# Retention scores and retained values as three fp32r passes of high and low parts, with two tiles moved in memory

## The chip, the cores and the metric

One core of a Trainium2 chip runs the whole program in one launch. The metric is the device time in microseconds (us). TensorE multiplies; its products land in eight PSUM banks. VectorE (DVE), ScalarE (ACT) and GpSimd (POOL) work on tiles in SBUF, and the queue of SyncE (SP) issues most transfers. Each engine takes its own instructions strictly in the order in which they are written.

## The reference

The model is an encoder trunk over two requests, a prompt of 256 and a sample of 512 tokens, 1024 wide, with two layers. Layer 0 mixes by retention, layer 1 by neighbourhood attention; each is followed by a mixture of 16 experts and a gated embedding. What the change touches is the retention mixer, here without the chunks in which the reference writes it:

```python
q, k, v, g = split(h @ w_in)                 # 4 heads; q, k 256 wide, v, g 512 wide
q = rope(q); k = rope(k) * 256 ** -0.5
scores = (q @ k.T) * decay                   # decay falls with the distance, both directions
o = scores @ v
o = (o - mean(o)) * rsqrt(var(o) + 1e-6) * gn_w
out = (silu(g) * o) @ w_out
```

## The kernel before

The retention stage is the first, at about 40 to 700 us. Its work is cut into eight units, one for each head and request, in the order of `UNITS` (line 33): units 0, 2, 4 and 7 are prompt units (2 tiles of 128 tokens), units 1, 3, 5 and 6 sample units (4 tiles). Weights come in chunks through `raw`; ScalarE casts a chunk to fp32r, its high part (`high_of_chunk`, line 604), and VectorE subtracts that from the original, which gives the low part (`low_of_chunk`, line 613). A dense product is then made of three fp32r matmuls, high by high, low by high, high by low (`part_products`, line 1443). A chunk's parts lie in one of two places, so that its cast waits until TensorE has used the chunk before the last.

For each unit TensorE runs, in this order: values (`two_chunks("v", ...)`, line 1480), scores (line 1485), the first half of the gates (`g0`, line 1490), the retained values `o` (line 1499), the second half of the gates (`g1`) with the transposes of the gated rows between its tiles (line 1506), the next unit's queries and keys (line 1519), and the unit's output (`o0`, `o1`, line 1527). Scores and `o` go through `product` (line 1375) in plain fp32; all other products of the stage through `part_products`. In units 0 and LAST (7) transposes of normed rows stand before and after the scores (`norm_columns`), and in LAST the router's logits and the choice of the experts' tokens for the sample (`eight_best`) lie between the steps.

The other engines have hand-written orders of their own. ScalarE (lines 1062 to 1116) casts chunks, copies values from PSUM to `r_v` (line 1091), takes the SiLU of the gates (line 1104) and casts the transposed rows (line 1067). VectorE (lines 1976 to 2047) subtracts low parts, turns queries and keys (`rotary`, line 1839) straight into `r_qk`, scales scores by the decay strip into `r_s` (`decayed`, line 1855), takes mean and variance of `o` (`centred`), multiplies by the gates into `r_og` (`gated`), subtracts for the low part of the transposed rows (`transposed`, into `r_ot`), and adds outputs to `resid` (`added`). `scaled` and `norm_low` make normed rows and their low parts, behind squares on ScalarE (line 1015) and roots on GpSimd (lines 858 and 859). PSUM banks are dealt in turn over the list of `ret_keys` (line 151): a product waits until the product eight places before it has been read out.

Of the kernel before, what the change touches and what calls it, by code (L numbers as in the profile page):

```python
# [21 lines left out]
P = 128  # L22
D = 1024
# [248 lines left out]
def build(nc, x_prompt, x_sample, p_prompt, p_sample, ret_w_in, ret_decay_logit, ret_gn_w, ret_w_out,  # L272
# [4 lines left out]
    with ctx:  # L277
# [29 lines left out]
        xn_first = [put(f"xn_first{t}", [P, D], 64 + 4 * t) for t in range(TT)]  # L307
        xn_mid = [put(f"xn_mid{t}", [P, D], kb) for t, kb in enumerate((176, 180, 60, 68, 168, 192))]
# [6 lines left out]
        r_qk = put("r_qk", [P, 4, SEQ_S], 48)  # L315
        r_v = put("r_v", [P, 4, RET_DV], 56)
        r_s = put("r_s", [P, 4, SEQ_S], 64)
        r_ot = [put(f"r_ot{k}", [P, 4, SEQ_S], 72 + 8 * k, F32R) for k in range(2)]
# [180 lines left out]
        ret_rot = sem("ret_rot")  # L499
# [495 lines left out]
        def _(act):  # L995
# [58 lines left out]

            for t in range(2):
                squares(0, t)
# [5 lines left out]
            for u in range(len(UNITS)):  # L1062
# [19 lines left out]
                if u == 0:  # L1082
                    squares(0, 4)
                    squares(0, 5)
# [4 lines left out]
                for t in range(nt):  # L1089
                    b, done = filled(act, "ret", ("v", u, t))  # L1090
                    nc.scalar.copy(r_v[:, t, :], b[:, :]).then_inc(done, 1)
                if u in (0, LAST):
                    for t in GROUP_TILES[1]:
                        norm_high(int(u == LAST), t)
                split_ret("g1", u)
# [17 lines left out]
                if u < LAST:  # L1113
                    if new_head(u + 1):
# [251 lines left out]
        def _(pe):  # L1366
# [8 lines left out]
            def product(phase, key, lhs, rhs, i=0, m=P):  # L1375

                b, full = fill(pe, phase, key, i)
                n = rhs[0].shape[-1]
                for c, (x, y) in enumerate(zip(lhs, rhs)):
                    last = nc.tensor.matmul(b[0:m, 0:n], x, y, start=(c == 0), stop=(c == len(lhs) - 1))  # L1380
                last.then_inc(full, 1)

# [94 lines left out]
            for u in range(len(UNITS)):  # L1477
# [5 lines left out]
                pe.wait_ge(ret_rot, 2 * u + 2)  # L1483
                for t in range(nt):
                    product("ret", ("s", u, t), [r_qk[:, 2 + k, t * P:(t + 1) * P] for k in range(2)],
                            [r_qk[:, k, 0:n] for k in range(2)])
# [8 lines left out]
                for t in range(nt):  # L1495
                    drained(pe, "ret", ("v", u, t))
                    drained(pe, "ret", ("s", u, t))
                for t in range(nt):
                    product("ret", ("o", u, t), [r_s[:, k, t * P:(t + 1) * P] for k in range(nt)],
                            [r_v[:, k, :] for k in range(nt)])  # L1500
# [870 lines left out]
```

## Time and profile before

| | before |
|---|---|
| three runs | 2460.53, 2458.11, 2456.77 us; median 2458.11 |
| profiled execution | 2456.45 us, its span 2454.8 us |
| TensorE busy | 2367.5 us, 96% of the span |
| VectorE busy | 1742.6 us, 71% |
| ScalarE busy | 1337.0 us, 54% |
| GpSimd busy | 298.8 us, 12% |
| mean granted TensorE clock | 0.985 |

The profile is that of one execution. Busy shares are means over stages with different limits; what ended last in a stage is read from the chain of waits, which is followed back from the last instruction. Matmuls overlap one another, so the mean duration of one is longer than the pace at which they follow each other; the pace is read from the chain, whose pieces join without overlap.

### The profile page before, as it was taken

The numbers are of one execution on the slowest core, as the hardware profiler recorded it, in microseconds if no ns is written. First come the engines' busy times: TensorE is split into PE (matmuls) and PEld (weight loads), VectorE is DVE, ScalarE is ACT, GpSimd is POOL, SyncE is SP. The second block draws the span as 40 slices with busy tenths as digits, with TensorE's granted clock in tenths as the row PEclk, the third lists the DMA queues.
The fourth block names the chain that finished last, engine by engine and source line by source line (L and its number), as shares of the span: only waits on it lengthen the run. The fifth ranks groups of instructions, "written<-read, shape, count | busy, mean of one in ns | idle before, by whom it ended". The sixth has DMA issues, their size and how long they took to land.

```text
span 2454.8 us, 33887 instructions
## 1 busy us (share of the span) xinstructions
PE 2367.5 (96%) x11934; PEld 1934.6 (79%) x11934; DVE 1742.6 (71%) x1989; ACT 1337.0 (54%) x1454; POOL 298.8 (12%) x360
## 2 busy tenths in 40 slices
PE   8999999999979999999999999998889999999997
PEld 6878788687768888888878888886678888888876
DVE  6545455344679888888866677766578888888854
ACT  4223222222447777777764455444157777777762
POOL 1000000000111221112111101000111111121011
PEclk9999999999989999999999999998889999999999
DMA  6424324132499999999972533332599999999931
GB/s 235 132 72 126 108 96 149 59 107 72 157 345 395 389 392 392 394 389 390 388 193 56 134 102 99 93 93 73 170 339 393 392 394 390 389 392 392 356 125 43
DMA packets 210961, 577.27 MB, mean 235 GB/s; under 512 B 24384, under 2 KB 65856, under 8 KB 210752
## 3 DMA queue, kind: packets, MB, share of 16 engines
q1 hardware_dynamic: 193584, 526.35, 57.5%
q0 software_dynamic: 17296, 49.83, 8.0%
q8 instruction: 53, 0.87, 0.1%
q14 instruction: 28, 0.23, 0.0%
HBM read 547.80 MB, written 30.43 MB: 236 GB/s over the span
## 4 chain that ended last, share of the span: by engine, by line
PE 91%; DVE 3%; DMA 3%; issue 1%; ACT 1%; POOL 0%; SPq 0%; DVEq 0%; POOLq 0%; ACTq 0%
PE bank L1557 43%; PE bank L1443 38%; PE bank L1372 4%; PE bank L1380 4%; PE bank L1743 1%; PE bank L1725 1%; DMA rows_normed<-xn_late 1%; DVE d_parts L613 1%; DMA m_x<-rows_normed,idx_t 1%; DMA resid<-in_x_sample 0%; DMA rows_summed<-m_y,idx_out 0%; DMA raw<-in_ret_w_in 0%; DVE top_i L1946 0%; DVE m_at L1948 0%; DMA resid<-rows_summed 0%
## 5 line engine op out<-in xcount | busy, mean ns | idle before, releaser
L2080 DVE TENSOR_TENSOR w_parts<-wt,w_parts 128x2048 fp32r<-128x2048 f32 x384 | 874.5, 2289 | 133.7 <-ACT w_parts L1133 125.3
L1133 ACT CAST w_parts<-wt 128x2048 fp32r<-128x2048 f32 x384 | 734.2, 1913 | 195.0 <-PE bank L1557 184.4
L1557 PE MATMUL bank<-w_parts,m_xt 128*128 128x512 f32 x2976 | 689.0, 390 | 2.1 <-ACT m_y L1191 2.1
L1557 PEld LDWEIGHTS bank<-w_parts,m_xt 128*128 128x128 f32 x2976 | 556.1, 188 | 117.2 <-issue 2.9
L1443 PE MATMUL bank<-d_parts,xt 128*128 128x512 f32 (+1 forms) x1872 | 388.0, 364 | 4.4 <-DVE d_parts L613 4.4
L1557 PE MATMUL bank<-w_parts,m_hidt 128*128 128x512 f32 x1632 | 382.7, 394 | 2.8 <-DVE m_hidt L2072 2.8
L1443 PEld LDWEIGHTS bank<-d_parts,xt 128*128 128x128 f32 x1872 | 316.0, 190 | 62.3 <-issue 7.4
L1557 PEld LDWEIGHTS bank<-w_parts,m_hidt 128*128 128x128 f32 x1632 | 306.1, 189 | 66.0 <-issue 3.3
L604 ACT CAST d_parts<-raw 128x512 fp32r<-128x512 f32 (+1 forms) x168 | 183.3, 1107 | 245.5 <-PE bank L1443 237.4
L613 DVE TENSOR_TENSOR d_parts<-raw,d_parts 128x512 fp32r<-128x512 f32 (+1 forms) x168 | 215.5, 1296 | 134.8 <-ACT d_parts L604 134.3
L1443 PE MATMUL bank<-xt,d_parts 128*128 128x256 f32 (+1 forms) x1536 | 284.1, 340 | 7.0 <-DVE xt L1803 2.9
L1443 PEld LDWEIGHTS bank<-xt,d_parts 128*128 128x128 f32 x1536 | 235.4, 189 | 37.5 <-issue 8.0
L1443 PE MATMUL bank<-e_w,xt 128*128 128x512 f32 x576 | 133.6, 391 | 0.0
L1443 PE MATMUL bank<-d_parts,r_ot 128*128 128x512 f32 x576 | 132.3, 390 | 0.0
L1443 PEld LDWEIGHTS bank<-d_parts,r_ot 128*128 128x128 f32 x576 | 107.6, 188 | 22.9 <-DVE r_ot L1891 0.2
L1443 PEld LDWEIGHTS bank<-e_w,xt 128*128 128x128 f32 x576 | 107.3, 188 | 21.9
L905 POOL DMA_INDIRECT m_x<-rows_normed,idx_in x26 | 86.6, 3330 | 21.9 <-POOL idx_in L902 19.5
L2242 DVE CUSTOM_DVE_ANT_0 n_s<-bank,n_b 128x256 f32<-128x256 f32 (+1 forms) x96 | 44.6, 465 | 57.6 <-PE bank L1725 55.4
L902 POOL COPY idx_in<-idx_t 96x1 uint32 x26 | 19.6, 755 | 531.1 <-PE bank L1372 531.1
L858 POOL TENSOR_SCALAR meansq<-mv 128x1 f32<-128x1 f32 x24 | 4.6, 192 | 551.5 <-DVE mv L1871 551.5
L1104 ACT ACTIVATE r_tmp<-bank 128x512 f32<-128x512 f32 x24 | 14.4, 599 | 102.9 <-PE bank L1443 102.9
L1380 PE MATMUL bank<-r_v,r_s 128*128 128x512 f32 x160 | 70.2, 593 | 0.0
(184 smaller groups left out, 2035.6 us busy)
## 6 DMA issues: line engine op xcount, KB each, us to landing
wt<-in_exp_w_gate SPq DMA_DIRECT2D x128, 1024.0 KB, 14.2
wt<-in_exp_w_up SPq DMA_DIRECT2D x128, 1024.0 KB, 13.1
wt<-in_exp_w_down SPq DMA_DIRECT2D x128, 1024.0 KB, 13.3
raw<-in_ret_w_in SPq DMA_DIRECT2D x32, 1024.0 KB, 5.2
raw<-in_na_w_in SPq DMA_DIRECT2D x24, 1024.0 KB, 5.4
raw<-in_ret_w_in SPq DMA_DIRECT2D x32, 512.0 KB, 4.5
raw<-in_ret_w_out SPq DMA_DIRECT2D x16, 1024.0 KB, 5.1
raw<-in_ple_w_gate SPq DMA_DIRECT2D x8, 1024.0 KB, 8.1
```

Source lines behind the costliest of these rows:

```text
L604: nc.scalar.copy((d_parts[:, b, 0, :] if dst is None else dst)[:, cols], raw[:, b, cols]).then_inc(part_h, 1)
L613: nc.vector.tensor_tensor(low[:, cols], raw[:, b, cols], high[:, cols].bitcast(F32), ALU.subtract)\
L905: nc.gpsimd.indirect_dma_start(out=m_x[:, :], out_offset=None, in_=rows_normed[l], in_offset=bass.IndirectOffsetOnAxis(ap=rows, axis=0)).t ...
L1133: nc.scalar.copy(w_parts[c % RING][:, 0, :], wt[:, place // 2, place % 2 * 2048:place % 2 * 2048 + 2048])\
L1372: last = nc.tensor.transpose(b[:, c * w:(c + 1) * w], src, ident[0:k, 0:k])
L1380: last = nc.tensor.matmul(b[0:m, 0:n], x, y, start=(c == 0), stop=(c == len(lhs) - 1))
L1443: ins = nc.tensor.matmul(b[0:m, 0:rhs.shape[-1]], lhs, rhs, start=(first and j == 0 and wk == xk == 0), stop=(last and j == tiles - 1 and ...
L1557: last = nc.tensor.matmul(b[:, :], lhs[x][:, 2 * k + j, :], w[:, part, j, f * HALF:(f + 1) * HALF], start=(k == j == 0 and x == part == 0) ...
L1725: last = nc.tensor.matmul(b[:, 0:nk * P], n_qk[qk][rows, h // 2, t * P:(t + 1) * P], n_qk[kk][rows, 2 + h // 2, k0 * P:(k0 + nk) * P], sta ...
L1743: last[k] = nc.tensor.matmul(o_bank[k * NA_DH:(k + 1) * NA_DH, h // 2 * P:(h // 2 + 1) * P], n_v[:, k0 + j, (h + k) * NA_DH:(h + k + 1) * ...
L2080: v.tensor_tensor(w_parts[c % RING][:, 1, :], wt[:, k // 2, k % 2 * 2048:k % 2 * 2048 + 2048], w_parts[c % RING][:, 0, :].bitcast(F32), AL ...
L2242: v.tensor_tensor_reduce(out=n_s[:, u % 2, 0:w], in0=b[:, 0:w], in1=n_b[:, u % 2, 0:w], scale=-1.0, scalar=-3 * MASKED, op0=ALU.add, op1=A ...
```

## The change

Scores and retained values are made by `part_products` too, in three fp32r matmuls in place of one fp32 product, and `product` goes away. `rotary` writes `r_qk_full`; ScalarE casts it into `r_qk` (`queries_high`), VectorE subtracts (`queries_low`, in place, into `r_qk_low`). `decayed` writes `r_s_full`; ScalarE casts it tile by tile into `r_s[0]` (`scores_high`), VectorE subtracts in place into `r_s[1]` (`scores_low`). The values' copy becomes a cast into `r_v[0]`, and VectorE subtracts from the bank into `r_v[1]` (`values_low`), which now is what frees the bank. TensorE waits for `ret_qk_low` in place of `ret_rot`, and for `ret_s_low` in place of the emptied score banks. In memory `r_ot` moves to the places of `r_s`, `r_qk_full` and `r_qk_low` share those of `r_og`, and two tiles each of `xn_first` and `xn_mid` move.

```diff
-        xn_first = [put(f"xn_first{t}", [P, D], 64 + 4 * t) for t in range(TT)]
-        xn_mid = [put(f"xn_mid{t}", [P, D], kb) for t, kb in enumerate((176, 180, 60, 68, 168, 192))]
+        xn_first = [put(f"xn_first{t}", [P, D], kb) for t, kb in enumerate((64, 68, 72, 76, 60, 84))]
+        xn_mid = [put(f"xn_mid{t}", [P, D], kb) for t, kb in enumerate((176, 180, 60, 84, 168, 192))]
...
-        r_qk = put("r_qk", [P, 4, SEQ_S], 48)
-        r_v = put("r_v", [P, 4, RET_DV], 56)
-        r_s = put("r_s", [P, 4, SEQ_S], 64)
-        r_ot = [put(f"r_ot{k}", [P, 4, SEQ_S], 72 + 8 * k, F32R) for k in range(2)]
+        r_qk = put("r_qk", [P, 4, SEQ_S], 48, F32R)
+        r_qk_low = [[put(f"r_qk_low{g}{j}", [P, 2, GROUPS[g][1]], 184 + (2, 8)[g] * j, F32R) for j in range(2)]
+                    for g in range(2)]
+        r_v = [put(f"r_v{k}", [P, 4, RET_DV], (56, 80)[k], F32R) for k in range(2)]
+        r_s = [put(f"r_s{k}", [P, 4, SEQ_S], 64 + 8 * k, F32R) for k in range(2)]
+        r_qk_full = [[put(f"r_qk_full{g}{j}", [P, 2, GROUPS[g][1]], 184 + (2, 8)[g] * j) for j in range(2)]
+                     for g in range(2)]
+        r_s_full = put("r_s_full", [P, 4, SEQ_S], 72)
+        r_ot = [put(f"r_ot{k}", [P, 4, SEQ_S], 64 + 8 * k, F32R) for k in range(2)]
...
# ScalarE
+            def queries_high(u):
+                g, n = unit(u)[1], unit(u)[3]
+                for j in range(2):
+                    act.wait_ge(ret_rot, 2 * u + j + 1)
+                    nc.scalar.copy(r_qk[:, 2 * j:2 * j + 2, 0:n], r_qk_full[g][j][:, :, :])\
+                        .then_inc(ret_qk_high, 1)
+            def scores_high(u):
+                n, nt = unit(u)[3:]
+                for t in range(nt):
+                    drained(act, "ret", ("s", u, t))
+                    nc.scalar.copy(r_s[0][:, t, 0:n], r_s_full[:, t, 0:n]).then_inc(ret_s_high, 1)
...
                 split_ret("v1", u)
                 if u == 0:
+                    queries_high(0)
                     squares(0, 4)
                     squares(0, 5)
...
                 for t in range(nt):
-                    b, done = filled(act, "ret", ("v", u, t))
-                    nc.scalar.copy(r_v[:, t, :], b[:, :]).then_inc(done, 1)
+                    b, _ = filled(act, "ret", ("v", u, t))
+                    nc.scalar.copy(r_v[0][:, t, :], b[:, :]).then_inc(ret_v_high, 1)
                 if u in (0, LAST):
                     for t in GROUP_TILES[1]:
                         norm_high(int(u == LAST), t)
+                scores_high(u)
                 split_ret("g1", u)
...
                 split_ret("o1", u)
                 if u < LAST:
+                    queries_high(u + 1)
                     if new_head(u + 1):
                         strip_exp(u + 1)
                     split_ret("v0", u + 1)
...
# TensorE
-                pe.wait_ge(ret_rot, 2 * u + 2)
+                pe.wait_ge(ret_qk_low, 2 * u + 2)
+                queries = [r_qk[:, 0:2, 0:n], r_qk_low[g][0]]
+                keys = [r_qk[:, 2:4, 0:n], r_qk_low[g][1]]
                 for t in range(nt):
-                    product("ret", ("s", u, t), [r_qk[:, 2 + k, t * P:(t + 1) * P] for k in range(2)],
-                            [r_qk[:, k, 0:n] for k in range(2)])
+                    part_products([x[:, :, t * P:(t + 1) * P] for x in keys], lambda k, a, j: queries[k][:, j, :], "ret",
+                                  [("s", u, t)], 2, lambda a: slice(0, P), True, True)
...
                 for t in range(nt):
                     drained(pe, "ret", ("v", u, t))
-                    drained(pe, "ret", ("s", u, t))
+                pe.wait_ge(ret_s_low, tiles_before(u) + nt)
                 for t in range(nt):
-                    product("ret", ("o", u, t), [r_s[:, k, t * P:(t + 1) * P] for k in range(nt)],
-                            [r_v[:, k, :] for k in range(nt)])
+                    part_products(r_v, lambda k, a, j: r_s[k][:, j, t * P:(t + 1) * P], "ret", [("o", u, t)], nt, None,
+                                  True, True)
...
# VectorE: rotary writes r_qk_full[g][j], decayed writes r_s_full; new:
+            def queries_low(u):
+                g, n = unit(u)[1], unit(u)[3]
+                for j in range(2):
+                    dve.wait_ge(ret_qk_high, 2 * u + j + 1)
+                    v.tensor_tensor(r_qk_low[g][j][:, :, :], r_qk_full[g][j][:, :, :], r_qk[:, 2 * j:2 * j + 2, 0:n].bitcast(F32), ALU.subtract)\
+                        .then_inc(ret_qk_low, 1)
+            def values_low(u):
+                for t in range(unit(u)[4]):
+                    b, done = filled(dve, "ret", ("v", u, t))
+                    dve.wait_ge(ret_v_high, tiles_before(u) + t + 1)
+                    v.tensor_tensor(r_v[1][:, t, :], b[:, :], r_v[0][:, t, :].bitcast(F32), ALU.subtract).then_inc(done, 1)
+            def scores_low(u):
+                n, nt = unit(u)[3:]
+                for t in range(nt):
+                    dve.wait_ge(ret_s_high, tiles_before(u) + t + 1)
+                    v.tensor_tensor(r_s[1][:, t, 0:n], r_s_full[:, t, 0:n], r_s[0][:, t, 0:n].bitcast(F32), ALU.subtract)\
+                        .then_inc(ret_s_low, 1)
...
                 low_ret("v1", u)
                 if u == 0:
+                    queries_low(0)
...
                 low_ret("g0", u)
+                values_low(u)
...
                 decayed(u)
+                scores_low(u)
                 low_ret("g1", u)
...
                 for t in range(nt):
                     added(u, t, 0)
+                queries_low(u + 1)
                 low_ret("v0", u + 1)
...
             low_ret("g0", LAST)
+            values_low(LAST)
             for t in (4, 5):
                 scaled(1, t)
...
             for t in (4, 5):
                 norm_low(1, t)
+            scores_low(LAST)
             low_ret("g1", LAST)
```

## Rows read from the trace of the kernel before

**Rows 1.** The page: busy times, and the chain that ended last.
```profile
PE 2367.5 (96%) x11934; PEld 1934.6 (79%) x11934; DVE 1742.6 (71%) x1989; ACT 1337.0 (54%) x1454; POOL 298.8 (12%) x360
...
PE 91%; DVE 3%; DMA 3%; issue 1%; ACT 1%; POOL 0%; SPq 0%; DVEq 0%; POOLq 0%; ACTq 0%
PE bank L1557 43%; PE bank L1443 38%; PE bank L1372 4%; PE bank L1380 4%; PE bank L1743 1%; PE bank L1725 1%; DMA rows_normed<-xn_late 1%; DVE d_parts L613 1%; DMA m_x<-rows_normed,idx_t 1%; DMA resid<-in_x_sample 0%; DMA rows_summed<-m_y,idx_out 0%; DMA raw<-in_ret_w_in 0%; DVE top_i L1946 0%; DVE m_at L1948 0%; DMA resid<-rows_summed 0%
```

**Rows 2.** Chain in order of time, units 2 to 4: start us, us, what.
```profile
239.37 43.58 PE bank L1443 x192
282.95 6.87 PE bank L1380 x16
289.82 10.89 PE bank L1443 x48
300.71 13.73 PE bank L1380 x32
...
326.34 0.61 ACT r_tmp L1104
...
327.08 5.99 PE bank L1443 x48
...
371.93 1.73 PE bank L1380 x8
```

**Rows 3.** Groups by shape: line, operation, count, busy us, mean ns, idle before.
```profile
L1443 PEld LDWEIGHTS bank<-d_parts,xt 128*128 128x128 f32 x1872 | 316.0, 190 | 62.3 <-issue 7.4 <-DVE d_parts L613 4.8
...
L1443 PE MATMUL bank<-d_parts,r_ot 128*128 128x512 f32 x576 | 132.3, 390 | 0.0
...
L1380 PE MATMUL bank<-r_v,r_s 128*128 128x512 f32 x160 | 70.2, 593 | 0.0
L613 DVE TENSOR_TENSOR d_parts<-raw,d_parts 128x512 fp32r<-128x512 f32 x104 | 68.9, 683 | 0.5 <-ACT d_parts L604 0.5
L604 ACT CAST d_parts<-raw 128x512 fp32r<-128x512 f32 x104 | 61.0, 611 | 1.0 <-DMA raw<-in_na_w_in 1.0
...
L2221 DVE TENSOR_TENSOR xt<-n_ot,xt 128x1024 fp32r<-128x1024 f32 x6 | 7.2, 1221 | 2.6 <-ACT xt L1304 2.6
L1304 ACT CAST xt<-n_ot 128x1024 fp32r<-128x1024 f32 x6 | 6.0, 1043 | 0.0
```

**Rows 4.** Prompt unit 4, first gated row (timeline) and its transposes (chain).
```profile
386.51 0.74 DVE L1883 SCALAR_TENSOR_TENSOR r_og<-r_og,mvr,r_tmp 128x512 f32<-128x512 f32 x1
...
388.00 0.44 PE bank L1372 x4
```

**Rows 5.** Timeline of VectorE and ScalarE, from unit 2 to unit 3.
```profile
255.30 1.28 DVE L1898 TENSOR_TENSOR resid<-resid,bank 128x512 f32<-128x512 f32 x2
257.70 2.29 DVE L613 TENSOR_TENSOR d_parts<-raw,d_parts 128x2048 fp32r<-128x2048 f32 x1 [1.12 <-ACT d_parts L604]
...
255.76 1.91 ACT L604 CAST d_parts<-raw 128x2048 fp32r<-128x2048 f32 x1 [3.53 <-PE bank L1443]
```

**Rows 6.** Unit 0: timeline of VectorE, then a piece of the chain.
```profile
57.57 2.48 DVE L1803 TENSOR_TENSOR xt<-bank,xt 128x512 fp32r<-128x512 f32 x4
60.20 2.29 DVE L613 TENSOR_TENSOR d_parts<-raw,d_parts 128x2048 fp32r<-128x2048 f32 x1
...
67.12 0.43 PE bank L1372 x4
```

**Rows 7.** Timeline of VectorE and ScalarE in the last unit.
```profile
641.28 2.48 DVE L1793 SCALAR_TENSOR_TENSOR xn_mid<-resid,rstd,gain 128x1024 f32<-128x1024 f32 x2
...
665.96 0.68 DVE L1937 COPY m_at<-bank 16x512 f32<-16x512 f32 x1 [0.55 <-PE bank L1424]
...
642.57 0.59 ACT L1091 COPY r_v<-bank 128x512 f32<-128x512 f32 x1 [2.13 <-PE bank L1443]
```

**Rows 8.** Chain, first piece of the first expert's products.
```profile
717.23 12.49 PE bank L1557 x48
```

**Rows 9.** Chain, a later piece of the expert stage.
```profile
764.47 16.40 PE bank L1557 x72
```

More of the change, by code:

```diff
@@ L498, in build @@
         strip_arg, strip_set = sem("strip_arg"), sem("strip_set")
-        ret_rot = sem("ret_rot")
+        ret_rot, ret_qk_high, ret_qk_low = sem("ret_rot"), sem("ret_qk_high"), sem("ret_qk_low")
+        ret_v_high, ret_s_high, ret_s_low = sem("ret_v_high"), sem("ret_s_high"), sem("ret_s_low")
         ret_var, ret_rstd, ret_og = sem("ret_var"), sem("ret_rstd"), sem("ret_og")
@@ L1373, in transposes @@
                 last.then_inc(full, 1)
[L1375 to L1381, printed above, removed]
             def keep_busy(phase, key, n):
@@ L1849, in rotary @@
                     v.tensor_tensor(t3, b[:, 0:n], cos_t[:, 0:n], ALU.mult).then_inc(done, 1)
-                    chain.link(v.tensor_tensor(r_qk[:, 2 * j, 0:n], t0, t1, ALU.subtract))
+                    turned = r_qk_full[unit(u)[1]][j]
+                    chain.link(v.tensor_tensor(turned[:, 0, :], t0, t1, ALU.subtract))
                     drained(dve, "ret", ("qk", u, 2 * j + 1))
-                    v.tensor_tensor(r_qk[:, 2 * j + 1, 0:n], t2, t3, ALU.add).then_inc(ret_rot, 1)
+                    v.tensor_tensor(turned[:, 1, :], t2, t3, ALU.add).then_inc(ret_rot, 1)
                     dve.wait_ge(ret_rot, 2 * u + j + 1)
+            def queries_low(u):
[15 more added lines that the diff above has]
+                        .then_inc(ret_s_low, 1)
             def decayed(u):
@@ L1860, in decayed @@
                     b, done = filled(dve, "ret", ("s", u, t))
-                    v.scalar_tensor_tensor(out=r_s[:, t, 0:n], in0=b[:, 0:n], scalar=RET_DK ** -0.5,
+                    v.scalar_tensor_tensor(out=r_s_full[:, t, 0:n], in0=b[:, 0:n], scalar=RET_DK ** -0.5,
                                            in1=r_strip[:, STRIP0 - t * P:STRIP0 - t * P + n],
```

## The prediction

> **What bounds the kernel now.** I read the page first. TensorE is busy for 96% of the span and carries 91% of the chain that ended last; VectorE carries 3% [rows 1]. The two fp32 products that the change rewrites, line 1380, are only 4% of that chain, about 98 us, so whatever the change gives must come out of those 98 us. They stand at about 58 to 662 us, in the retention stage. There the chain of waits in order of time is almost one unbroken run of TensorE pieces [rows 2]: in the four sample units (4 tiles of 128 tokens) the only other link is a 0.61 us SiLU, once per unit. So in that stage a microsecond taken off TensorE is a microsecond off the end, unless something else then comes late. After the stage each pass over an expert's half is again one TensorE piece of 16.40 us [rows 9], so what is won earlier is carried through.
>
> **What leaves and what comes on TensorE.** The price is the pace in the chain, not the mean of one, because matmuls overlap: the mean of one fp32 instruction is 593 ns [rows 3], but 32 of them take 13.73 us, 0.429 us each [rows 2]. The trace shows 32 instructions for the 16 products of a sample unit's `o`, two per product.
> - fp32 product of 512 columns: 13.73/16 = 0.858 us. Of 256 columns: the prompt units' `s`, 1.73/4 = 0.433 us [rows 2].
> - fp32r matmul with a new weight load each time, which is what `part_products` issues: 512 columns 10.89/48 = 0.227 us, 256 columns 5.99/48 = 0.125 us [rows 2]. Three of them: 0.681 and 0.374 us.
> - So 0.177 us is saved per product of 512 columns and 0.058 us per product of 256.
> - Sample unit: `s` has 4 x 2 = 8 products, `o` has 4 x 4 = 16: 24 x 0.177 = 4.25 us. Prompt unit (2 tiles): `s` 4 of 256 columns, `o` 4 of 512: 4 x 0.058 + 4 x 0.177 = 0.94 us.
> - Four units of each kind: 17.0 + 3.8 = 20.8 us.
>
> **What comes on ScalarE and VectorE.** Per unit: two casts of the turned queries and keys and two subtractions, one cast and one subtraction for each tile of scores, one subtraction for each tile of values (the values' copy was there and only changes its type). From rows of the same shapes [rows 3]: cast of 128x1024 1.04 us, of 128x512 0.61; subtraction of 128x1024 1.22, of 128x512 0.68. For 128x256 the line through each pair gives 0.41 and 0.39, as estimates. A sample unit's VectorE gets 2 x 1.22 + 8 x 0.68 = 7.9 us more, beside some 80 us; a prompt unit's about 3.6. VectorE is busy for under half of the stage, so the sum fits; what matters is where each lies. The moves of tiles within memory (`r_ot` over `r_s`, the remainders over `r_og`, `xn_first`, `xn_mid`) issue nothing, and every place is read out before by the order of the products; I cost them at nothing.
>
> Scores to outputs. TensorE's wait changes from the decayed scores to `ret_s_low`. After the last score tile come decay, cast, subtraction: 0.69 + 0.61 + 0.68, about 2.2 us with handovers in a sample unit, and 0.41 + 0.39 + 0.41 and a tile's backlog, about 1.6 us in a prompt unit. Between `s` and `o` TensorE has the first half of the gates, 10.89 us and in a prompt unit, with half the tiles, 5.45 [rows 2]. Cost nothing, with 3.8 us in hand in the tighter kind. Behind these steps the gates' second cast on ScalarE and its subtraction are queued; in a prompt unit the scores' casts end 1.15 us after the scores, and 1.91 + 2.29 us (the durations in [rows 5]) make it 5.4, while TensorE asks at 5.45 + 2.73 = 8.2. Nothing.
>
> Scaling the outputs in a prompt unit. `o` gets 0.7 us shorter, while VectorE's chain to the first gated row starts from the end of the first gates (cast and subtraction of the next chunk, then `centred`) and does not move. Before, that row was done at 386.51 + 0.74 = 387.25 and its transposes ran from 388.00 [rows 4]: 0.75 us in hand, all used up. Units 2 and 4: 0, at most 0.3 each. Sample units have `centred` under four longer tiles: nothing.
>
> Next unit's values. VectorE does `queries_low` ahead of the `v0` subtraction, and behind it wait that chunk and TensorE. The tight place is prompt to sample (units 0, 2, 4), where the output stage is short. At unit 2 the two additions end at 256.58 and the `v0` subtraction started at 257.70 after an idle 1.12 us [rows 5]. With 2 x 1.22 us ahead of it, and 0.07 to 0.08 us of overlap between neighbours as the start times show, it runs from about 258.8 to 261.1. TensorE asks for it at 239.37 + 96 x 0.227 = 261.16 [rows 2]. The slack of about 1.2 us becomes almost nothing: I take 0.1 us for each of three, bounds 0 and 1.0. On ScalarE `queries_high` ends near 254.3, before the `v0` cast at 255.76 [rows 5]: nothing. In the other four crossings the output stage is twice as long: nothing.
>
> Unit 0. ScalarE now holds the squares of tiles 4 and 5 behind `queries_high(0)`, which waits for the rotation; their normed rows come some 2.5 us later, and TensorE, which wants them only behind the unit's values and scores, still has about 6 us in hand. But `scores_high` lies ahead of the `g1` cast, which so starts 0.66 us later; behind it `norm_low(4, 5)` ended at 57.57 + 2.48 = 60.05 and let the next chunk's subtraction start at 60.20 [rows 6]. Followed through the queue, that start goes to 60.6, and the first gated row with it from 66.4 to 66.8. Its transposes ran at 67.12 [rows 6]; TensorE, 0.94 us earlier, would now ask at 66.2: 0.6 us lost.
>
> Last unit. `values_low` waits for the second value tile's copy (642.57 + 0.59) before `scaled(1, 4)` and `(1, 5)`, which started at 641.28 and now start at 643.8; `norm_low(2, 3)` follows after 2.48 us, from 646.2 instead of 643.7 [rows 7]. The transposes of tile 5 use the banks that it empties, so TensorE stands for about 0.6 us, of which 0.23 was won in `s`: 0.35 us lost. From 665.96 VectorE leads the chain (the choice of the eight best), and it starts on TensorE's `affinities`, so it comes 0.6 us earlier, no more.
>
> Sum: 20.8 - 0.3 - 0.6 - 0.35 = 19.5 us. The profiled execution took 2456.45 us (span 2454.8); less 19.5 it is 2436.9. It lies 1.66 us under the median of the three runs, 2458.11, so against the median I forecast **2438.6 us**.
>
> **A rule weighed.** Each of the new matmuls has a weight load of its own, and a load takes 190 ns [rows 3], which is most of the time between two matmuls. In this trace 48 matmuls with 48 loads take 0.227 us each, even 0.125 us with 256 columns [rows 2], so loads lie under the matmuls. The Trainium skill, "TensorE: Matmul & The Clock Gate", section "The mechanism", says that a load overlaps with running matmuls only if they use other row groups, which full 128-row tiles don't; by that rule the load would be added to each matmul and the change would come out as rival 1 has it. The trace disagrees with it.
>
> **The rivals.**
> 1. The loads come into the open in the new products (here both operands are scratch tiles, not weights). 384 matmuls x 0.19 us = 73 us against 20.8: 2458.1 + 53 = 2511 us, slower. It decides from 20.8/384 = 54 ns of open load for each matmul. Against it: the paces of 0.227 and 0.125 us in [rows 2]; the second is shorter than one load, so loads there lie wholly under other work.
> 2. Three passes cost what the fp32 product did. By the means of one this is so: 2 x 593 = 1186 ns against 3 x 390 = 1170 [rows 3]. Then only the stalls of 1.25 us and some 1 us of gain are left: about 2458, no change. Against it: TensorE's pieces of the chain, which give 0.858 and 0.681.
> 3. The queues give half back: VectorE's additional steps delay the `v0` chunk by their whole 2.44 us at the three prompt-to-sample crossings (7.3 us), and the prompt units, whose slack behind `o` is used up, return their 3.8 us: 20.8 - 11.1 = 9.7, so 2448. For it: both places have almost no slack left. Against it: VectorE's idle 1.12 us in front of `v0` [rows 5].
>
> **How the numbers follow.** Forecast 0.86, rival 3 0.08, rival 2 0.03, rival 1 0.03. The forecast's own bounds: best, no stall at all and 1.5 us less of the slow pace with which the experts begin (48 matmuls took 12.49 us there [rows 8], against 10.9 in the stage before): 2458.1 - 22.3 = 2435.8, and 1.7 more for the lower of the runs; worst, 1.0 us at each of the three crossings, all 3.8 us of the prompt units lost (the losses in units 0 and last within these) and 1.5 us more of that slow pace: 20.8 - 8.3 = 12.5, so 2445.6. Range **2434 to 2446**. Faster by over 0.2% (4.9 us, about what a measurement of this kernel can tell from no change): 0.86 + 0.08 = 0.94; same 0.03; slower 0.03.
>
> **What would show it.** Right: in the sample units `s` is a piece of 5.45 us and `o` one of 10.9; TensorE does not wait for the scores' remainders; unit 0's and the last unit's transposes wait 0.6 us each; the expert stage begins 19 to 20 us earlier and keeps its pieces of 16.40. Wrong: pieces of `s` and `o` over 6 and 12 us (rivals 1 and 2), or TensorE waiting for `v0`'s parts at the prompt-to-sample crossings for over 1 us (rival 3).

## The result, and the profile after

The changed kernel takes 2442.20 us (median; 2440.67 to 2442.81) against 2457.86 us for the kernel before (2456.77 to 2460.53): a ratio of 0.9935 with a 95% interval of 0.9923 to 0.9947, 15.7 us less. In a later comparison it was 2440.45 against 2458.54 us, 0.9931 (0.9917 to 0.9944). The forecast was 2438.6 us, 19.5 us less, with a range of 2434 to 2446.

The page of the profile after, beside [rows 1]: busy times, and the chain that ended last. TensorE loses 13.9 us of busy time, VectorE gains 41.3 and ScalarE 25.2, and the line of fp32 products (1380 before) is gone; `part_products` is now line 1459, transposes are line 1396.

```profile
PE 2353.6 (96%) x12062; PEld 1959.1 (80%) x12062; DVE 1783.9 (73%) x2053; ACT 1362.2 (56%) x1494; POOL 299.5 (12%) x360
...
PE 90%; DVE 4%; DMA 3%; issue 1%; ACT 1%; POOL 0%; SPq 0%; DVEq 0%; POOLq 0%; ACTq 0%
```

The chain in order of time over units 2 and 3 (start us, us, what), the place of [rows 2]:

```profile
189.97 23.46 PE bank L1459 x109
...
220.83 0.75 DVE r_og L1925
221.59 0.04 issue
221.63 0.66 PE bank L1396 x4
222.29 10.92 PE bank L1459 x48
233.21 0.44 PE bank L1396 x4
233.64 76.46 PE bank L1459 x336
```

What were the four pieces at the head of [rows 2] (outputs and values, `s`, gates, `o`) and the 24 matmuls of the second gates behind them is one piece of 336 matmuls at 76.46/336 = 0.2276 us each, the pace that the prediction took from 10.89/48. The new links are in the prompt unit, from ScalarE and VectorE, ending at the gated row of 220.83; they come back below. The timeline of TensorE shows a sample unit's `s` by itself (start, us, engine, line, operation, tiles): its 24 matmuls run from 277.30 to the next product at 282.74, 5.44 us, where the prediction wanted 5.45.

```profile
277.30 0.39 PE L1459 MATMUL bank<-r_qk 128*128 128x512 f32 x1
...
282.74 1.52 PE L1459 MATMUL bank<-d_parts,xt 128*128 128x512 f32 x6
```

Groups by shape over the retention stage, beside [rows 3] (count, busy us, mean ns, idle before). The added steps cost what rows of the same shapes said; the estimates for 128x256, 0.41 us for the subtraction and 0.39 for the cast, measured 421 and 414 ns. Beside each matmul lies a load of 188 ns.

```profile
L1459 PE MATMUL bank<-r_v,r_s 128*128 128x512 f32 x240 | 56.0, 390 | 0.0
L1459 PEld LDWEIGHTS bank<-r_v,r_s 128*128 128x128 f32 x240 | 45.0, 188 | 9.4
L1894 DVE TENSOR_TENSOR r_s<-r_s_full,r_s 128x512 fp32r<-128x512 f32 x16 | 10.0, 685 | 0.0
L1074 ACT CAST r_s<-r_s_full 128x512 fp32r<-128x512 f32 x16 | 9.9, 622 | 14.9 <-DVE r_s_full L1903 14.9
L1879 DVE TENSOR_TENSOR r_qk_low<-r_qk_full,r_qk 128x1024 fp32r<-128x1024 f32 x8 | 9.4, 1220 | 0.0
L1066 ACT CAST r_qk<-r_qk_full 128x1024 fp32r<-128x1024 f32 x8 | 8.1, 1051 | 0.0
L1894 DVE TENSOR_TENSOR r_s<-r_s_full,r_s 128x256 fp32r<-128x256 f32 x8 | 3.0, 421 | 1.9 <-ACT r_s L1074 1.6
L1074 ACT CAST r_s<-r_s_full 128x256 fp32r<-128x256 f32 x8 | 3.0, 414 | 2.5 <-DVE r_s_full L1903 2.5
```

The waits of TensorE's matmuls from 60 to 640 us (waiting line, releaser: us in total, times, longest) name neither the scores' remainders nor the `v0` chunk. Its weight loads do wait for that chunk, 0.33 us at each of the three prompt-to-sample crossings; this comes back below.

```profile
PE bank L1459 <- ACT r_tmp L1127: 1.4, 4, 0.3
PE bank L1396 <- DVE xt L1821: 0.5, 1, 0.5
PE bank L1396 <- DVE r_og L1925: 0.4, 1, 0.4
```

The first expert's products begin at 698.08 us in place of 717.23 [rows 8], 19.15 us earlier, and later pieces keep their length [rows 9]:

```profile
698.08 12.89 PE bank L1575 x48
710.97 0.66 PE bank L1396 x8
711.63 16.38 PE bank L1575 x72
```

So 19.15 us were won at that point, and the two profiled spans (2454.8 and 2439.0 us) differ by 15.8. The experiments ask two things: whether the 19 us are made of what the prediction says, and where 3.4 us of them went behind it.

For that I cut every profile at the same places: the start of each unit's values on TensorE (for unit 0 the second half of them, 24 matmuls, from 39.63 us before, which the table calls its first), the end of the last unit's output, the first expert product, and, at the end of the attention stage, the stretch from its last dense 128x256 product to the first transposes of the third normed rows (`xn_late`). All in us:

| | unit 0, its first 24 matmuls | sample unit 3 | prompt unit 2 | last unit | from there to experts | first values to experts | attention's end | span |
|---|---|---|---|---|---|---|---|---|
| before | 60.96, 7.90 | 99.86 | 60.58 | 50.87 | 34.87 | 677.60 | 56.05 | 2454.8 |
| after | 60.16, 7.29 | 95.69 | 59.92 | 50.95 | 34.63 | 658.44 | 58.65 | 2439.0 |
| only `o` | 60.48, 7.37 | 96.99 | 60.11 | 50.95 | 35.23 | 665.13 | 56.81 | 2444.8 |
| only scores | 61.22, 8.40 | 98.55 | 60.37 | 50.55 | 35.24 | 672.12 | 56.85 | 2452.7 |
| no subtractions | 60.74, 7.94 | 95.56 | 59.80 | 49.87 | 34.86 | 657.62 | 56.61 | 2438.2 |
| after, idle transposes | 60.73, 7.86 | 95.69 | 59.92 | 50.95 | 33.97 | 658.41 | 54.89 | 2436.6 |
| after again | 60.22, 7.36 | 95.67 | 59.91 | 50.94 | 34.82 | 658.74 | 55.52 | 2435.8 |
| before, idle transposes | 60.21, 7.17 | 99.86 | 60.58 | 50.87 | 34.08 | 676.03 | 54.86 | 2454.0 |
| after, other order in the last unit | 60.22, 7.34 | 95.73 | 59.91 | 49.91 | 35.61 | 658.53 | 56.06 | 2438.7 |
| after, other order and idle transposes | 60.15, 7.29 | 95.68 | 59.90 | 49.87 | 35.52 | 658.23 | 54.86 | 2437.4 |
| before, second | 60.35, 7.34 | 99.86 | 60.60 | 50.86 | 35.04 | 677.17 | 56.04 | 2453.3 |
| before, third | 60.36, 7.31 | 99.86 | 60.58 | 50.87 | 34.12 | 676.21 | 56.04 | 2453.8 |
| after, third | 59.95, 7.11 | 95.69 | 59.89 | 50.94 | 35.11 | 658.71 | 55.81 | 2435.5 |
| after, fourth | 60.17, 7.34 | 95.67 | 59.90 | 50.96 | 35.44 | 659.29 | 56.57 | 2437.3 |

### The profile page after: what moved, and what is told of

Read it like the earlier page. It is cut to its first block, busy times and chain, and to the rows that moved or that the text cites. A ratio compares the mean times of both kernels' runs of the same rounds, so it can differ in the third digit from the quotient of the medians.

```text
span 2439.0 us, 34267 instructions
## 1 busy us (share of the span) xinstructions
PE 2353.6 (96%) x12062; PEld 1959.1 (80%) x12062; DVE 1783.9 (73%) x2053; ACT 1362.2 (56%) x1494; POOL 299.5 (12%) x360
## 4 chain that ended last, share of the span: by engine, by line
PE 90%; DVE 4%; DMA 3%; issue 1%; ACT 1%; POOL 0%; SPq 0%; DVEq 0%; POOLq 0%; ACTq 0%
PE bank L1575 43%; PE bank L1459 40%; PE bank L1396 4%; PE bank L1761 1%; PE bank L1743 1%; DMA rows_normed<-xn_late 1%; DVE d_parts L619 1%; DMA m_x<-rows_normed,idx_t 0%; DMA rows_summed<-m_y,idx_out 0%; DMA resid<-in_x_sample 0%; DMA raw<-in_ret_w_in 0%; ACT d_parts L610 0%; DVE top_i L1988 0%; DMA resid<-rows_summed 0%; DVE m_at L1990 0%
## 5 line engine op out<-in xcount | busy, mean ns | idle before, releaser
L911 POOL DMA_INDIRECT m_x<-rows_normed,idx_in x26 | 86.5, 3327 | 21.9 <-POOL idx_in L908 19.5
L908 POOL COPY idx_in<-idx_t 96x1 uint32 x26 | 19.6, 754 | 531.6 <-PE bank L1396 531.6
L1347 ACT ACTIVATE n_p<-n_s,nmx 128x256 f32<-128x256 f32 (+1 forms) x96 | 52.4, 546 | 36.5 <-DVE nmx L2290 20.7
L1340 ACT COPY n_pt<-bank 128x256 f32<-128x256 f32 (+1 forms) x48 | 19.6, 408 | 85.1 <-PE bank L1396 85.1
## 6 DMA issues: line engine op xcount, KB each, us to landing
wt<-in_exp_w_up SPq DMA_DIRECT2D x128, 1024.0 KB, 12.5
```

The costliest lines, as they stand in the source:

```text
L911: nc.gpsimd.indirect_dma_start(out=m_x[:, :], out_offset=None, in_=rows_normed[l], in_offset=bass.IndirectOffsetOnAxis(ap=rows, axis=0)).t ...
L1347: nc.scalar.activation(n_p[:, u % 2, 0:w], n_s[:, u % 2, 0:w], ACT.Exp, bias=nmx[:, u % 2:u % 2 + 1], scale=-1.0, accum_out=den[:, t % 2, ...
```

## The experiments

My theory was that TensorE's passes are the gain, product by product. Against it stood the rivals that the gain lies in one of the two products only, that the extra steps on ScalarE and VectorE take part of it back, and, for the 3.4 us behind the experts, that the change costs TensorE clock at the end of the attention stage.

**Only `o` in three passes.** Scores stay one fp32 product of `r_qk`, without high and low parts of queries and keys.

```diff
-                pe.wait_ge(ret_qk_low, 2 * u + 2)
+                pe.wait_ge(ret_rot, 2 * u + 2)
...
-                    part_products([x[:, :, t * P:(t + 1) * P] for x in keys], lambda k, a, j: queries[k][:, j, :], "ret",
-                                  [("s", u, t)], 2, lambda a: slice(0, P), True, True)
+                    product("ret", ("s", u, t), [r_qk[:, 2 + k, t * P:(t + 1) * P] for k in range(2)],
+                            [r_qk[:, k, 0:n] for k in range(2)])
```

> Only the retained values o are made in three passes; scores stay a plain fp32 product, queries and keys have no low parts. Theory (the gain is TensorE's, by the pace of its pieces): 4 x 2.83 + 4 x 0.71 = 14.2 us leave the retention stage, less 0.3 to 0.8 in the first and the last unit, so the experts' first products begin 13.4 to 13.9 us before those of the kernel before (717.23 us there), and o in a sample unit is a run of 10.9 us. Total 13.5 us under before (2444.4), or up to 2.7 us less where the clock falls early at the end of the attention. Rival (three passes cost what the fp32 product did, and the gain of the change came from the scores or the waits): under 3 us.

It took 2445.20 us against 2458.00, ratio 0.9948 (0.9935 to 0.9962). A sample unit fell from 99.86 to 96.99 us, 2.87; a prompt unit by 0.47, where 0.71 was expected, and the last unit by nothing. From the first values to the experts it is 677.60 - 665.13 = 12.5 us less, under the expected 13.4 to 13.9. Its chain in unit 3 (lines are two lower here: 1394 is the fp32 product, 1457 `part_products`) has the scores as before, while `o` has melted into a piece of 120 matmuls at 27.22/120 = 0.227 us:

```profile
279.63 6.87 PE bank L1394 x16
286.50 27.22 PE bank L1457 x120
313.71 0.44 PE bank L1386 x4
```

**Only the scores in three passes.** `o` stays one fp32 product of `r_s_full` and the copied values, without scores' and values' remainders; `r_ot` and the normed rows stand where they stood before.

```diff
-                pe.wait_ge(ret_s_low, tiles_before(u) + nt)
...
-                    part_products(r_v, lambda k, a, j: r_s[k][:, j, t * P:(t + 1) * P], "ret", [("o", u, t)], nt, None,
-                                  True, True)
+                    product("ret", ("o", u, t), [r_s_full[:, k, t * P:(t + 1) * P] for k in range(nt)],
+                            [r_v[0][:, k, :] for k in range(nt)])
```

> Only the scores are made in three passes; o stays a plain fp32 product, values and scores have no low parts. Theory: 4 x 1.42 + 4 x 0.23 = 6.6 us leave the retention stage, and nothing is lost in the last unit, where nothing is put ahead of the normed rows: the experts begin at 710.4 to 710.9 us against 717.23. Total 6.6 us under before (2451.3), or up to 2.7 less. With the run of o alone the two must add up to 20 to 20.8 us in the stage, if neither part needs the other. Rival: under 2 us.

It took 2452.52 us against 2458.00, ratio 0.9976 (0.9967 to 0.9985). A sample unit fell by 1.31 us, a prompt unit by 0.21. From the first values to the experts it is 677.60 - 672.12 = 5.5 us less, where 6.3 to 6.8 were expected; 0.5 of what is missing is at the 24 matmuls at the start, 8.40 us in this profile against 7.90. Its chain in unit 3 (fp32 products on line 1396) keeps `o` at 13.73 us, as in [rows 2]:

```profile
269.84 31.05 PE bank L1459 x137
300.89 13.73 PE bank L1396 x32
314.63 5.46 PE bank L1459 x24
```

The parts add up. In a sample unit 2.87 + 1.31 = 4.18, and the whole change gives 99.86 - 95.69 = 4.17; in a prompt unit 0.47 + 0.21 = 0.68 against 0.66; over units 1 to 6 together 12.43 + 5.80 = 18.23 against 18.21. Both products pay, in a sample unit by about the number of products, 16 and 8. The expected 20 to 20.8 us for both over the whole stage were not reached: 12.5 + 5.5 = 18.0, against 19.2 in the first pair. The 1.2 us between them lie outside units 1 to 6, where profiles of one kernel differ by as much (677.60 and 676.21 before).

**All passes, no subtractions.** VectorE's remainders of queries, keys, values and scores are left out, TensorE reads the high parts in their place. With them goes VectorE's reading of the values' banks, which ScalarE's cast frees again, as in the kernel before.

```diff
-                pe.wait_ge(ret_qk_low, 2 * u + 2)
-                queries = [r_qk[:, 0:2, 0:n], r_qk_low[g][0]]
-                keys = [r_qk[:, 2:4, 0:n], r_qk_low[g][1]]
+                pe.wait_ge(ret_qk_high, 2 * u + 2)
+                queries = [r_qk[:, 0:2, 0:n], r_qk[:, 0:2, 0:n]]
+                keys = [r_qk[:, 2:4, 0:n], r_qk[:, 2:4, 0:n]]
...
-                queries_low(u + 1)
...
-                values_low(u)
...
-                scores_low(u)
```

> The changed kernel with all its passes on TensorE and all its casts on ScalarE, but without the subtractions on VectorE: where a low part was read, the high part is read again, so the products lack their low parts and the outputs are only coarse. Theory (VectorE's new steps cost only where they stand ahead of normed rows: 0.4 us in unit 0, 0.85 in the last unit): the experts begin 19.6 to 20.2 us before those of before, against 18.75 us for the whole change. Rival (VectorE's steps eat into the gain in each unit): 22 us or more earlier.

It took 2439.92 us against 2458.00, ratio 0.9926 (0.9913 to 0.9940). From the first values to the experts it is 677.60 - 657.62 = 20.0 us less than before, within the expected 19.6 to 20.2 and well under the rival's 22; the whole change gives 19.2. VectorE is busy for 1743.0 us here, 40.9 less than after, and yet units 1 to 6 together take 512.15 us against 512.70: the subtractions cost TensorE 0.55 us there. What they do cost is in the last unit, 49.87 against 50.95 us. The prompt units stay at 59.80: of the 0.28 us that they lack of the predicted 0.94, more than half is not from the remainders.

**Idle transposes at the end of the attention stage**, in the changed kernel and in the kernel before. In the profile after, the stretch there was 2.60 us longer than in the profile of before, at a lower granted clock. The edit gives TensorE transposes of the identity there, which nothing reads, and touches nothing in the retention stage. The changed kernel ran unchanged beside them.

```diff
+                        if phase == "nal" and u == 24:
+                            keep_busy(phase, ("pt", u - 2), 30)
                         if h == 0:
                             o_bank
...
+                        if phase == "nal" and v >= 13:
+                            keep_busy(phase, ("pt", v), 4)
                         pe.wait_ge(na_weights, at(v + 1, len(units), q))
```

> The changed kernel with idle transposes on TensorE in the gaps of the last attention steps (4 in front of each of the last eleven transposes of weights, 30 in the longest gap). Theory (the missing 2.7 us go where TensorE's granted clock falls to half during these sparse steps, some 19 us earlier in the work than before): the clock stays up, the stretch from the step after the last full products to the first normed transposes (68.4 us before, 71.0 after) takes 66 to 68 us, total 2.5 to 4.5 us under the changed kernel (2442.2), about 2438.5. Rival (VectorE or a transfer holds that stretch, and the clock is only a sign of it): 71 us again, total within 1 us of the changed kernel, or slower by the work added.

> The changed kernel once more, for its stage times and its stretch at the attention's end beside those of the next three. Theory (the retention stage's gain is fixed by TensorE's pieces, while what the clock takes at the attention's end differs from one execution to the next): units 1 to 6 within 0.1 us of the first look (95.7, 59.9, 95.7, 59.9, 106.0, 95.6), the stretch anywhere from 55 to 59 us (58.65 in the first look). Rival (the loss there belongs to the changed kernel): 58 to 59 us again.

> The kernel before with the same idle transposes on TensorE at the attention's end. Theory of the clock: its stretch goes from 56.05 to 54.9, as in the changed kernel with them, total 1 to 2 us under before. Then the change's gain between the two kernels with idle transposes is the retention stage's 18.6 to 19.2 us. Rival (the clock loss belongs to the change): the kernel before gains nothing or loses by the added work.

The changed kernel with idle transposes took 2438.37 us, ratio 0.9924 (0.9911 to 0.9938) to before; unchanged 2440.45, ratio 0.9931 (0.9917 to 0.9944); the kernel before with them 2455.99 against 2458.54, ratio 0.9993 (0.9984 to 1.0002), so that by the times alone a gain from them isn't proven. The profiles say more. The stretch is cut into windows of 14 us from the last dense product on (length, busy us and count of each engine, granted clock as a share of 2.4 GHz, share of the transfers, GB/s). Here is the second window, first in after, then in the same kernel again:

```profile
1651.40:1665.40 14.00, 8.72 (x52) 6.39 (x52) 7.16 (x26) 4.94 (x14) 0.56 (x1) 0.50 0.30 110
```

```profile
1652.40:1666.40 14.00, 7.76 (x62) 5.72 (x63) 8.32 (x26) 6.09 (x16) 0.61 (x1) 0.81 0.29 111
```

A granted clock of 0.50 is the lower of the two levels, 1.2 GHz, for the whole window; the chain shows how long the same 12 products take there, in after and in the same kernel again:

```profile
1651.56 1.55 PE bank L1761 x12
1653.10 1.47 PE bank L1396 x6
```

```profile
1652.46 0.88 PE bank L1761 x12
1653.33 0.82 PE bank L1396 x6
```

One kernel, two executions: 58.65 and 55.52 us for the stretch, and with it spans of 2439.0 and 2435.8. With idle transposes all windows of the stretch have a granted clock of 1.00, and it takes 54.89 and 54.86 us in the two kernels; the second window of the changed one:

```profile
1654.80:1668.80 14.00, 11.95 (x116) 10.42 (x117) 8.01 (x26) 5.78 (x16) 0.56 (x1) 1.00 0.29 111
```

With the stretch alike, the two kernels differ by 17.4 us in span and 17.6 in their medians; the two were measured on different chips, with the kernel before at 2458.00 and 2458.54 us beside them.

**Whether the change itself costs clock there** needed more executions of both kernels, unchanged.

> The kernel before, unchanged, for one more profile. The stretch at the end of the attention stage, from the end of its last dense 128x256 product to the first transposes of the third normed rows, took 56.05 us in the profile of before, 58.65 and 55.52 us in the two profiles of the changed kernel, and 54.86 to 54.89 us wherever idle transposes kept TensorE at work. Theory A (the granted clock in this stretch differs by execution, in both kernels alike): 55 to 59 us here, with no order between the kernels. Theory B (the changed kernel loses more clock there because of the change): 55.5 to 56.2 us here and in the second look at before, and over 57 us in both looks at the changed kernel. From the start of the first values to the first expert product both give 677 to 678 us.

> The changed kernel, unchanged, for one more profile of the same stretch. Theory A: 55 to 59 us, with no order between the kernels. Theory B: over 57 us, and above both looks at before. From the start of the first values to the first expert product both give 658 to 659 us.

> A second profile of the kernel before. Theory A: the stretch takes 55 to 59 us. Theory B: 55.5 to 56.2 us.

> A second profile of the changed kernel. Theory A: the stretch takes 55 to 59 us. Theory B: over 57 us.

Their times were 2455.04 and 2455.49 us for the kernel before, 2437.24 and 2439.04 for the changed one; one more execution of the kernel before, without a profile, took 2459.14. The stretch took 56.04 and 56.04 us before, 55.81 and 56.57 after. Theory B falls: three of four executions of the changed kernel lie below 57 us, two below every one of before. Theory A holds in that no order stands between the kernels, but not in that both vary: before gave 56.05, 56.04, 56.04, the changed kernel 55.52 to 58.65. Why the one is steady and the other not stays open, with three and four profiles, which do not all come from one chip. In the changed kernel the stretch is the longer the lower the granted clock of its second window: 58.65 us at 0.50, 56.57 at 0.74, 55.81 and 55.52 at 0.81. The 2.60 us of the first pair are thus no constant cost; the medians of the stretch are 56.04 and 56.19.

**Another order in the last unit.** VectorE scales the rows of tiles 4 and 5 before it takes the values' remainders.

```diff
-            values_low(LAST)
             for t in (4, 5):
                 scaled(1, t)
+            values_low(LAST)
             for t in (2, 3):
                 norm_low(1, t)
```

> The changed kernel with the values' subtraction of the last unit moved behind the two scalings of normed rows. Theory (it holds back the scaling, then the low parts whose banks the transposes of tile 5 need): the wait of 0.5 us and the slow second half go, the last unit from its values to its output takes 50.0 to 50.4 us instead of 50.95, total 0.7 us under the changed kernel. Rival (VectorE's chain of the choice of experts sets that end whatever TensorE does): 50.9 again.

> Both: the last unit's order and the idle transposes at the attention's end, on the changed kernel. Theory: the two add up, 3.3 us (2.5 to 4.5) under the changed kernel of this same job, total about 2437.5. Rival: no more than the idle transposes alone, 2438.4.

With the order alone 2439.60 us, ratio 0.9921 (0.9907 to 0.9934); with idle transposes too 2439.42, ratio 0.9926 (0.9912 to 0.9940). Neither can be told from the unchanged kernel's 2440.45, where 0.7 and 3.3 us less were expected. The last unit is whole again, 49.91 us, but from there to the experts it takes 35.61, and the sum, 658.53, is as without the order. Where the microsecond goes can be followed. Counted from the first values, the sample's scores reach VectorE at 647.57 - 41.09 = 606.48 us here and at 647.10 - 39.57 = 607.53 in the unchanged kernel run beside it: 1.05 us earlier, so TensorE's gain does enter the choice, and VectorE's queue follows it at the same pace. It is lost at the router's logits for the prompt, whose 24 matmuls take 0.77 us longer. The timeline of TensorE there, first the unchanged kernel, then the one with the other order:

```profile
673.82 4.51 PE L1459 MATMUL bank<-xt,rw_parts 128*16 128x256 f32 x24 [2.45 <-DVE xt L1821]
```

```profile
674.34 5.28 PE L1459 MATMUL bank<-xt,rw_parts 128*16 128x256 f32 x24 [3.12 <-DVE xt L1821]
```

and the window of 672 to 680 us (columns as above), in the same order:

```profile
672.00:680.00 8.00, 4.80 (x26) 3.25 (x26) 5.69 (x15) 1.62 (x2) 0.00 (x0) 0.79 1.03 422
```

```profile
672.00:680.00 8.00, 5.28 (x24) 3.28 (x24) 5.60 (x12) 0.34 (x1) 0.00 (x0) 0.50 1.01 410
```

So small a gain would also fit a choice whose start VectorE sets by itself, but the copy 1.05 us earlier speaks against that. The granted clock was 0.50 in that window, the lower level throughout. With both edits the same 24 take 5.26 us, but the fourth profile of the unchanged kernel has 5.16 too, at 0.59, and the run with only `o`, which keeps the order, has 5.28 at 0.50 as well. So the low clock there doesn't need the other order; whether the order makes it more likely stays open. No version measured beats the changed kernel beyond the scatter; the lowest median, 2438.37 us, is the one with idle transposes alone.

## Why the prediction was right, and where its sizes were off

The sign, the mechanism and the range were right. Summed by the medians of three profiles before and four after, from the first values to the first expert product, it was 677.17 - 658.73 = 18.4 us, where the forecast had 19.5. The steps whose size was wrong are the last unit's wait and the slack of the prompt units; unit 0's loss came out by luck. Point by point:

| | predicted | measured |
|---|---|---|
| unit 0: 0.94 - 0.6 - 0.1 | 0.24 | 60.36 - 60.17 = 0.2 |
| four sample units | 17.0 | 4.18 + 4.17 + 4.21 + 4.31 = 16.9 |
| prompt units 2 and 4, a crossing off each | 1.68 | 0.66 + 0.67 = 1.33 |
| last unit: 0.94 - 0.35 | 0.59 | 50.87 - 50.95 = -0.1 |
| from there to the experts | 0 | 34.87 - 34.97 = -0.1 |

- **The price of a product** held to a hundredth: 0.227 us per matmul, with loads under it. Rival 1 (2511 us) and rival 2 (2458 us) fall with the piece of 336. The Trainium skill's rule in "TensorE: Matmul & The Clock Gate", "The mechanism", that a load overlaps only with matmuls on other row groups, is again not what the trace shows: 188 ns of load lie under each 227 ns. In the same section, ahead of that rule, the Trainium skill also has loads into a background weight buffer pulled ahead of running matmuls; no run here shows where a load went.
- **Casts and subtractions** took what rows of their shapes said, and TensorE never waited for the scores' remainders, as predicted.
- **The prompt-to-sample crossing** came out nearly as worked: VectorE's idle 1.12 us of [rows 5] is filled by `queries_low`, the `v0` subtraction ends at 253.06 + 2.29 = 255.35, and the first weight load of the new unit, which had waited 0.33 us for it, starts at 255.40 (timeline of the loads, last line below). The piece of 336 around it is 76.46 us, and without subtractions it is 76.19. So a crossing with what follows it in the unit costs at most 0.27 us (0.1 was forecast), and rival 3, which wanted 2.44, falls.

```profile
250.79 2.35 DVE L1879 TENSOR_TENSOR r_qk_low<-r_qk_full,r_qk 128x1024 fp32r<-128x1024 f32 x2
253.06 2.29 DVE L619 TENSOR_TENSOR d_parts<-raw,d_parts 128x2048 fp32r<-128x2048 f32 x1
...
255.40 6.87 PE L1459 MATMUL bank<-d_parts,xt 128*128 128x512 f32 x29
...
255.40 2.60 PEld L1459 LDWEIGHTS bank<-d_parts,xt 128*128 128x128 f32 x12 [0.33 <-DVE d_parts L619]
```

- **The prompt units** lost 0.2 us each at the first gated row. The step "0.75 us in hand, all used up" read 388.00 from the chain [rows 4], whose pieces are cut so that they don't overlap. The timeline of before, below, starts those transposes at 387.84, under the tail of the gates' last matmul: 387.84 - 387.25 = 0.59 us were in hand, against 0.71 won in `o`. After, the second line, they start at 377.24, behind the gated row and past the tail, and the chain's piece of four is 0.65 us in place of 0.44. The timeline of TensorE in unit 4, first before, then after:

```profile
387.84 0.60 PE L1372 MATMUL bank<-ident,r_og 128*128 128x128 f32 x4
```

```profile
371.59 5.60 PE L1459 MATMUL bank<-d_parts,xt 128*128 128x512 f32 x24
377.24 0.65 PE L1396 MATMUL bank<-ident,r_og 128*128 128x128 f32 x4
```

- **Unit 0** lost at its first gated row what was forecast, 0.6 us, but by luck. The row is best compared with the second profile of before, whose 24 matmuls at the start took 7.34 us, where after has 7.29 (timelines of VectorE and TensorE below, first that profile, then after). The forecast put the row 0.4 us later; it is 0.08 later. The forecast had some 0.7 us in hand, from the chain's 67.12; by the timeline it was 66.35 - 65.76 = 0.59. With TensorE 0.94 us earlier, 0.94 - 0.59 + 0.08 = 0.43 us of waiting are left, of which the trace has 0.40, and 0.23 more go for a piece that no longer overlaps its neighbour (0.66 against 0.43 in [rows 6]). So a delay taken too long made up for slack read too large and for an overlap that the sum didn't have. The 0.8 us of gain that unit 0 shows in the first pair are mostly not the change's: the 24 matmuls at its start took 7.90 us in that profile of before and 7.34 and 7.31 in the others.

```profile
65.02 0.74 DVE L1883 SCALAR_TENSOR_TENSOR r_og<-r_og,mvr,r_tmp 128x512 f32<-128x512 f32 x1
66.35 0.60 PE L1372 MATMUL bank<-ident,r_og 128*128 128x128 f32 x4
```

```profile
65.10 0.74 DVE L1925 SCALAR_TENSOR_TENSOR r_og<-r_og,mvr,r_tmp 128x512 f32<-128x512 f32 x1
65.90 0.66 PE L1396 MATMUL bank<-ident,r_og 128*128 128x128 f32 x4 [0.40 <-DVE r_og L1925]
```

- **The last unit** is the term that was mis-sized. Its transposes waited where the forecast said, for the banks that `norm_low` empties behind `values_low`. But the run of 16 stands in two halves now: from its start to the next product it takes 629.29 - 626.57 = 2.72 us, where before's timeline has 647.51 - 645.85 = 1.66, so 1.06 us more; against the run without subtractions the unit lost 50.95 - 49.87 = 1.08 us, not 0.6. The run of only `o`, which has `values_low` too, takes 50.95 as well, that of only scores, without it, 50.55. And the step took the 0.23 us won in `s` off that loss though the 20.8 had counted it already. So nothing of the unit's 0.94 was left for the experts' choice: the copy of the scores starts 18.91 us earlier than in [rows 7], 647.05 against 665.96, while the unit itself had started 631.49 - 612.50 = 18.99 us earlier. The timelines, first before, then after:

```profile
645.85 1.91 PE L1372 MATMUL bank<-ident,xn_mid 128*128 128x128 f32 x16
647.51 5.73 PE L1443 MATMUL bank<-d_parts,xt 128*128 128x512 f32 x24
```

```profile
626.57 1.04 PE L1396 MATMUL bank<-ident,xn_mid 128*128 128x128 f32 x8
628.10 1.16 PE L1396 MATMUL bank<-ident,xn_mid 128*128 128x128 f32 x8 [0.50 <-DVE xt L1821]
629.29 5.73 PE L1459 MATMUL bank<-d_parts,xt 128*128 128x512 f32 x24
...
647.05 0.68 DVE L1979 COPY m_at<-bank 16x512 f32<-16x512 f32 x1 [0.23 <-PE bank L1440]
```

- **Behind the experts' start** the sum had no term; only the range allowed 1.5 us either way for the slow pace of the experts' first 48 matmuls, which took 12.89 us in place of 12.49. Of the first pair's 3.4 us, 2.60 are the attention's end at a granted clock of 0.50, which other executions of the same kernel don't have; 0.5 are in the stretch from the first expert product to the attention's last dense product (938.81 before; 939.33, 940.14, 939.41 and 939.19 after, 938.87 and 938.96 in the other two of before), whose cause I have not looked for, and 0.25 lie behind the attention. Over all fourteen profiles the stretch between these two products takes 938.8 to 941.3 us, 939.21 in the kernel before with idle transposes, so the 0.5 are not shown to be the change's.
- **Readings of the working that were off** and changed nothing: the fp32 pieces begin at 49.28 us, not at 58. VectorE was busy for 339.59 us of the 650 from 40 to 690 us, 52%, where the working had under half, and for 45.19 us in sample unit 3, where it had some 80. Rival 1's 73 - 20.8 is 52, which gives 2510 us.

## What to carry to other kernels

Price a matmul by the pace of a long unbroken piece of the chain, with its number of passes: here that gave the sample units, 16.9 us measured, as 17.0. Read slack from the start times of the timeline rather than from the chain, whose pieces are cut at their overlaps, and count what a wait adds beyond its idle time: a piece that starts late no longer runs under its neighbour's tail, some 0.2 us here. A step put into a serial queue ahead of one that frees a bank delays it by its own length and by what the step itself waits for; TensorE loses what of that its slack doesn't cover, here 1.08 us in the last unit.

## What was not expected of the hardware

Where TensorE is sparse, the granted clock differed between executions of one kernel: 0.50 against 0.81 in windows of 14 us over the same work at the end of the attention stage, worth up to 3.1 us, and 0.59 against 0.79 at the prompt's logits, worth 0.65 (5.16 against 4.51 us). Transposes of the identity kept it at 1.00 in the first of these and the stretch within 0.05 us. The 24 matmuls at the start of unit 0 took 7.11 to 8.40 us over all profiles, 7.31 to 7.90 in three of one and the same kernel, so a difference of 0.6 us there is no sign of a change.
